# Projections of retention heads one to five as 2x2 blocks from seven products

## Chip, core and metric

One core of one Trainium2 chip. The metric is the device time of one launch in microseconds. Engines are named as in the profile: PE is TensorE (PEld its weight loads), DVE is VectorE, ACT is ScalarE, POOL is GpSimd, SP is SyncE, which here issues the DMAs.

## What is computed

A trunk of two layers over 1024 tokens of width 1024, all in float32. Layer 0 mixes tokens by retention (six heads of width 128), layer 1 by neighbourhood attention; in both, four memory heads of width 64 attend to 256 memory tokens. Each layer ends in a feed-forward part. The change lies in the input projection of layer 0:

```python
proj = a @ w_in                      # a: 1024 x 1024, normed tokens
q, k, v, g, mq = jnp.split(proj, [768, 1536, 2304, 3072], axis=-1)
qh = rotary(to_heads(q, 6), pos)
kh = rotary(to_heads(k, 6), pos) * 128 ** -0.5
vh = to_heads(v, 6)
# forward and backward scans over chunks of 128 tokens, with a decay per head
y = retention(qh, kh, vh, log_gamma[0]) + flipped retention(..., log_gamma[1])
y = group_norm(y) * gn_g + gn_b      # per head and token
y = silu(g) * y
m = memory_attention(mq, mem_k, mem_v)
return jnp.concatenate([y, m], axis=-1) @ w_out
```

## The kernel before

**Matmuls.** A float32 product is made of three fp32r matmuls (`three`, L2321 to L2325): high part by high, high by low, low by high. A high part is a rounded copy, made on ScalarE; the low part is the rest, made on GpSimd or VectorE.

**Units.** The projection goes in units: a unit n is 128 output features, its weight tile `stage[:, n % 3, :]` has 1024 columns (eight k tiles of 128). SyncE loads it (`load_units`, in a ring of three), ScalarE makes `whi` (`split_hi`), GpSimd `wlo` in two halves (`split_lo`, L929). `project(n, k)` multiplies it with k tile k of the tokens `aT` (th: token half 0 or 1, hi or lo), into one PSUM bank per token half. A unit is 8 x 2 x 3 = 48 matmuls of 512 columns. Units `U_RETH + 4h` to `+ 4h + 3` are query, key, value and gate of retention head h.

**Stages.** First the memory keys and values, then the memory queries. Then the memory attention of layer 0, in 19 steps (`mem_step`): sixteen tiles of 128 tokens and head pair go through scores, maxima (DVE, `memory_peaks`), exponentials (ACT), normalising (DVE, L2014), transposes (PE, L2596), copy (ACT) and product with the values. Between them TensorE works off the 32 k tiles of head 0's four units. VectorE also builds the decay tables there (`decays`) and rotates head 0's query and key.

**The head loop.** For h = 1 to 5 TensorE does: unit q of head h; `chunk_scores(h)`, which turns keys and values of head h-1 to token rows and makes its chunk scores; unit k; `chunk_states(h)`; unit v; `chunk_outputs(h)`; unit gate; `turn_outputs(h)`. All work of one head's chunks thus has a unit of the next head beside it. VectorE: `rotate` (query; four instructions per token half, the first three read PSUM), `values` (V and the decayed scores ST), `rotate` (key), `scan` (14 state updates), `take_scaled` (value), `group_norm`, `take_gate`, `gated_values`. ScalarE: the high parts, `Ktok` and `vfb` (keys and decayed values by rows), `Silu` of the gate, gain and offset of the group norm. GpSimd: the low parts, the decayed queries `qfb` (L1104) and the factors of the group norm.

**Order of the work.** It is written out by hand for each engine, in its own instruction queue; semaphores join them. There is no planner. An engine stops at each wait, and whatever is queued behind the waiting instruction stops with it.

**Room.** SBUF is full. `whi` and `wlo` (24 KB of a partition) are free while no unit is in them. After the last head `out_rows` begins the output projection, with the parts of the concatenation split in `cat_split`; heads 0 and 1 of it are split early, into `catE`.

Of the kernel before, what the change touches and what calls it, by code (L numbers as in the profile page):

```python
# [62 lines left out]


# [34 lines left out]
def trunk_program(nc, wpack, w1, w2, x, mem, x_cols, mem_cols, gains, gain_rows, gn, decay, rpb, ropes, decay_consts, na_masks, ident_c, out):  # L99
# [9 lines left out]
    memkv_dram = nc.dram_tensor("memkv_scratch", [P, 1536], F32).ap()  # L109
# [75 lines left out]
    W = X + 64 * KB  # L185
    W += 6 * KB
    bdK = at("bdK", [P, 2, 2 * MEM], F32, W + 53 * KB)
    memV = at("memV", [P, 2, 2 * P], F32, W + 57 * KB)
# [3 lines left out]
    ropeC = at("ropeC", [P, SEQ], F32, W)  # L192
    ropeS = at("ropeS", [P, SEQ], F32, W + 4 * KB)
    QD = at("QD", [P, 2, RH, P], F32, W + 8 * KB)
    DM = at("DM", [P, RH, P], F32, W + 14 * KB)
    qT = at("qT", [P, 2, SEQ], F32, W + 17 * KB)
    kT = at("kT", [P, SEQ], F32, W + 25 * KB)
    Ktok = at("Ktok", [P, 8, P], F32, W + 29 * KB)
    V = at("V", [P, 8, P], F32, W + 33 * KB)
    ST = at("ST", [P, 8, P], F32, W + 37 * KB)  # L200
    vT = at("vT", [P, SEQ], F32, W + 41 * KB)
    states = at("states", [P, 8, 2, P], F32, W + 45 * KB)
    catE = at("catE", [P, 2, 2, HALF], F32R, Z + 24 * KB)
    rawE = at("rawE", [P, 2, HALF], F32, Z + 32 * KB)
    rtmp = at("rtmp", [P, HALF], F32, Z + 36 * KB)
    dconst = at("dconst", [P, 6, P], F32, Z)
    dexp = at("dexp", [P, 2, P], F32, Z + 3 * KB)
    mvT = at("mvT", [P, 2, MEM], F32, W + 49 * KB)
    junk_first = at("junk_first", [P, D], BF16, W + 51 * KB)
    xraw = at("xraw", [P, 2, KD, HALF], F32, W + 17 * KB)  # L210
    memraw = at("memraw", [P, KD, MEM], F32, Z + 16 * KB)
    xrow = at("xrow", [P, SEQ], F32, X + 64 * KB)
    junk_dve = at("junk_dve", [P, D], BF16, Z + 34 * KB)
    memA = at("memA", [P, 2, KD, MEM], F32R, W)
    memrow = at("memrow", [P, MEM], F32, X + 68 * KB)
# [10 lines left out]
    with ExitStack() as ctx:  # L226
# [22 lines left out]
        s_in = [sem(f"s_in{r}") for r in range(6)]  # L249
        b_in = [[sem(f"b_in{b}_{c}") for c in range(3)] for b in range(4)]  # L250
# [5 lines left out]
        cat_ld = [[sem(f"cat_ld{th}_{k}") for k in range(KD)] for th in range(2)]  # L256
        cat_hi, cat_lo = sem("cat_hi"), sem("cat_lo")
# [8 lines left out]
        k_last = sem("k_last")  # L266
        v_mm, v_ea, v_ed = sem("v_mm"), sem("v_ea"), sem("v_ed")
# [18 lines left out]
        for n in range(4 * RH):  # L286
            taken_by(U_RETH + n, "d")
# [53 lines left out]
        def cat_source(l, th, k):  # L341

            if (l, th) == (0, 0) and k < 2:
                return rawE[:, k, :]
            return catf[:, k, HALF * th:HALF * th + HALF]
# [11 lines left out]

        RUN_A0 = (0, 16, 0, 0)
# [13 lines left out]
        def unit_bank(n):  # L372

            return 2 * (n % 2) + (4 if U_RETH + 4 <= n < U_OUT0 else 0)
# [74 lines left out]

        USED, count = {}, 0  # L450
        for n in range(U_END):
            for l in range(2):
# [86 lines left out]
        def s_come(l, q):  # L539
            return 16 * ((13, 13, 13, 13, 13, 12)[s_slot(q)] * l + q // 6 + 1)  # L540
# [9 lines left out]
        def _(sp):  # L550
            issued = [0]

            def load_units(upto):

                for n in range(issued[0], min(upto, U_END)):
                    if n >= RING:
                        sp.wait_ge(w_lo, n - RING + 1)
# [59 lines left out]
            def out_phase(l):  # L617

                U, e = U_OUT[l], 16 * l
                if l == 0:  # L620
                    load_units(U + 9)
                    sp.wait_ge(*USED[U + 4])
                    for i in range(2, TT):
                        load_h(i)
# [16 lines left out]
            def before_out(l):  # L641

                sp.wait_ge(oc_rdy, 16 if l else 2)
                for i in range(TT if l else 2):
                    load_h(16 * l + i)
                if l:
                    load_gain(2 * l)
                    return
                for k in range(2):
                    sp.wait_ge(oc_st[k], stored(k))  # L650
                    sp.dma_start(rawE[:, k, :], cat_dram[0, k, :, 0:HALF]).then_inc(cat_ld[0][k], 16)
# [6 lines left out]
            def cat_back(l, th, tiles, free=None):  # L658

                cols = slice(HALF * th, HALF * th + HALF)  # L660
                sp.wait_ge(*(free or USED[U_OUT[l] - 1]))
# [26 lines left out]
            def load_w1(l, m):  # L688

                if m < RING:  # L690
                    sp.wait_ge(w_lo, U_OUT[l] + 2 * KD - 2 + m)
                else:
                    w1_freed(l, m - RING)
# [109 lines left out]
            sp.dma_start(memkv_dram[:, 0:1024], bdK[:, :, :].rearrange("p a c -> p (a c)")).then_inc(mkv_st, 16)  # L803
            sp.dma_start(memkv_dram[:, 1024:1536], memV[:, :, :].rearrange("p a c -> p (a c)")).then_inc(mkv_st, 16)
# [8 lines left out]
            before_out(0)  # L813
            load_units(U_RETH + 4 + 5)
            for h in range(1, RH):
                load_units(U_RETH + 4 * h + 4 + 5)
                if h == 4:
                    sp.wait_ge(cat_lo, 2)
                    load_gain(0)
                if h == RH - 1:  # L820
                    cat_back(0, 0, range(2, KD - 2))
# [27 lines left out]
            sp.dma_start(bdK[:, :, :].rearrange("p a c -> p (a c)"), memkv_dram[:, 0:1024]).then_inc(mkv_ld, 16)  # L849
            sp.dma_start(memV[:, :, :].rearrange("p a c -> p (a c)"), memkv_dram[:, 1024:1536]).then_inc(mkv_ld, 16)  # L850
# [64 lines left out]
        def _(pool):  # L915
# [8 lines left out]
            def split_lo(n, slot, need):  # L924
                pool.wait_ge(w_hi, need)
                width = w_cols(n).stop // 2
# [6 lines left out]
            def los(upto):  # L933

                for n in range(done[0], min(upto, U_END)):
                    if n in (FIRST_LO, U_NA + 2):
                        pool.wait_ge(w_lo, n)
                    split_lo(n, w_slot(n), n + 1)
# [143 lines left out]
            pool.memset(bdK[:, :, :], 0.0).then_inc(zer, 1)  # L1082
# [10 lines left out]
            for h in range(RH + 1):  # L1093
                n = U_RETH + 4 * h
                los(min(n + 3, U_OUT0 + 2))
                if h == RH:
                    los(U_OUT0 + 3)
                if h:

                    pool.wait_ge(kv_mm, h)  # L1100
                    pool.wait_ge(*EV[n - 4])
                    pool.wait_ge(dec_e, 3)
                    for d in range(2):
                        ins = pool.tensor_tensor(qfb[:, d, :].rearrange("p (a c) -> p a c", a=8),  # L1104
                                                 qT[:, (h - 1) % 2, :].rearrange("p (a c) -> p a c", a=8),
                                                 QD[:, d, h - 1:h, :].to_broadcast([P, 8, P]), ALU.mult)
                    ins.then_inc(qfb_rdy, 1)
                    los(min(n + 5, U_OUT0 + 2) if h < RH else U_OUT0 + 4)

                    for b in range(2):  # L1110
                        four = slice(4 * b, 4 * b + 4)
                        pool.wait_ge(var_rdy, 2 * h - 1 + b)
                        link(pool.tensor_scalar(gvar[:, four], mv[:, four, 1], 1.0, 1e-5, ALU.mult, ALU.add))
                        pool.tensor_tensor(grstd[:, four], gvar[:, four], minus_half[:, four], ALU.pow).then_inc(grs_rdy, 1)
                if h < RH:
                    los(n + 6)
# [44 lines left out]
        def _(act):  # L1161
# [8 lines left out]
            def his(upto):  # L1170

                for n in range(done[0], min(upto, U_END)):
                    if U_NA <= n < U_NA + RING:
                        act.wait_ge(g_used, (71, 72, 73)[w_slot(n)])
                    split_hi(n, w_slot(n), w_come(n), USED[n - RING] if n >= RING else None)
# [206 lines left out]
            def out_hi(l, q):  # L1382
# [11 lines left out]
                if p in "123":  # L1394
                    act.wait_ge(b_in[BLOCK_OF[p]][k // 4], 16 * (l + 1))
# [89 lines left out]
            def cat_split(l, pieces):  # L1485

                for piece in pieces:
# [5 lines left out]
                    else:  # L1493

                        act.wait_ge(cat_ld[th][k], 16 * (l + 1))
# [41 lines left out]
            def take_value_gate(h, i):  # L1537

                n = U_RETH + 4 * h + i
                his(n + 3)  # L1540
                if i == 3:
                    act.wait_ge(*EV[n])
                    act.activation(OC[:, h % 2, :], OC[:, h % 2, :], ACT.Silu).then_inc(ev_act, 1)


            for t in range(steps(RUN_A0)):
                mem_step(RUN_A0, t)
                decays(t)
                for u in units_done(t, 4 * KD, steps(RUN_A0)):
                    take_value_gate(0, u)  # L1550
            for h in range(1, RH + 1):
                n = U_RETH + 4 * h
                g = h - 1
                if h < RH:
                    his(n + 3)
                for b in range(2):
                    act.wait_ge(ktr, 2 * h - 1 + b)
                    act.activation(Ktok[:, 4 * b:4 * b + 4, :].rearrange("p a c -> p (a c)"),
                                   PS[:, (4 if h == RH else 0) + b, :], ACT.Copy).then_inc(ktok_rdy, 1)
                act.wait_ge(vtr, h)  # L1560
                if h == 1:
                    act.wait_ge(dec_rdy, 2 + RH)
# [6 lines left out]
                if h < RH:  # L1569
                    his(n + 4)  # L1570
                    take_value_gate(h, 2)
                    if h == 3:
                        cat_split(0, range(2))
                    take_value_gate(h, 3)
# [1369 lines left out]
```

## Time and profile before

| | us |
|---|---|
| median of 3 runs (2225.1 to 2225.68) | 2225.38 |
| span of the profiled execution | 2224.7 |
| PE busy | 2211.3 |
| DVE busy | 1228.9 |
| POOL busy | 1086.9 |
| ACT busy | 889.0 |

The profiled execution has no time of its own beside its span; the median of the runs lies 0.7 us above that span. PE's busy time counts overlapped matmuls as modelled, so 99% says that it hardly ever waits and not that it can go no faster. The granted clock is full in all slices of the page. The memory attention of layer 0 lies at about 47 to 119 us, head 1 begins at 119 us, and the key transposes of the last head at 399 us.

### The profile page before, as it was taken

How to read it: one execution, taken by the hardware profiler on the slowest of the kernel's cores; microseconds unless marked ns; L12 is line 12 of the kernel's file. 1: busy time of each engine (PE TensorE's matmuls, PEld its weight loads, DVE VectorE, ACT ScalarE, POOL GpSimd, SP SyncE). 2: the span in 40 equal slices, each digit the busy share in tenths (PEclk: the TensorE clock that was granted, in tenths of full speed). 3: DMA queues.
4: the chain of work that ended last, by engine and by line, in shares of the span. 5: the costliest groups of instructions: out<-in, count | busy, mean ns of one | idle time of the engine just before them, and what ended most of it. 6: DMA issues, size and time to landing. Idle time of an engine off the chain costs nothing.

```text
span 2224.7 us, 31738 instructions
## 1 busy us (share of the span) xinstructions
PE 2211.3 (99%) x11662; PEld 1820.2 (82%) x11662; DVE 1228.9 (55%) x2075; ACT 889.0 (40%) x1775; POOL 1086.9 (49%) x881
## 2 busy tenths in 40 slices
PE   9999999999999999999999999999999999999998
PEld 8788888888888888888889877768878888888887
DVE  6744454647644444577763245555575344447767
ACT  6621111455232333344564345565732323324444
POOL 1133333478988888400325243416799888870001
PEclk9999999999999999999999999999999999999999
DMA  8021111443443333663363533234433433238334
GB/s 335 29 86 48 48 48 58 141 162 108 149 147 114 100 110 104 218 218 98 91 203 113 140 83 81 66 131 161 161 114 126 149 100 114 95 124 321 95 97 164
DMA packets 130968, 280.89 MB, mean 126 GB/s; under 512 B 31983, under 2 KB 46590, under 8 KB 128766
## 3 DMA queue, kind: packets, MB, share of 16 engines
q1 hardware_dynamic: 130814, 278.86, 37.6%
q8 instruction: 94, 1.54, 0.3%
q14 instruction: 60, 0.49, 0.1%
HBM read 208.03 MB, written 70.80 MB: 125 GB/s over the span
## 4 chain that ended last, share of the span: by engine, by line
PE 94%; POOL 3%; ACT 1%; DVE 1%; issue 1%; DMA 0%; SPq 0%; POOLq 0%; DVEq 0%; ACTq 0%
PE PS L2323 28%; PE PS L2325 28%; PE PS L2324 28%; PE PS L2596 2%; POOL OPS L993 2%; PE PS L2834 2%; PE PS L2816 1%; PE PS L2733 1%; PE PS L2583 1%; PE PS L2629 1%; POOL TW L1017 1%; PE PS L2720 0%; PE PS L2744 0%; PE PS L2748 0%; PE PS L2746 0%
## 5 line engine op out<-in xcount | busy, mean ns | idle before, releaser
L2323 PE MATMUL PS<-AOP,OPS 128*128 128x512 f32 x1216 | 474.5, 390 | 1.1 <-POOL OPS L993 0.6
L2325 PE MATMUL PS<-AOP,OPS 128*128 128x512 f32 x1216 | 473.4, 389 | 0.0
L2324 PE MATMUL PS<-AOP,OPS 128*128 128x512 f32 x1216 | 473.3, 389 | 0.0
L929 POOL TENSOR_TENSOR wlo<-stage,whi 128x512 fp32r<-128x512 f32 (+1 forms) x160 | 203.1, 1292 | 312.7 <-ACT whi L1168 312.5
L993 POOL TENSOR_TENSOR OPS<-TW,OPS 128x512 fp32r<-128x512 f32 x174 | 263.2, 1527 | 78.9 <-ACT OPS L1266 77.6
L2323 PEld LDWEIGHTS PS<-AOP,OPS 128*128 128x128 f32 x1216 | 228.3, 188 | 51.2 <-POOL OPS L993 2.4
L2325 PEld LDWEIGHTS PS<-AOP,OPS 128*128 128x128 f32 x1216 | 228.3, 188 | 47.5
L2324 PEld LDWEIGHTS PS<-AOP,OPS 128*128 128x128 f32 x1216 | 228.3, 188 | 47.1
L2323 PE MATMUL PS<-aT,whi 128*128 128x512 f32 x640 | 261.7, 409 | 0.0
L2325 PE MATMUL PS<-aT,wlo 128*128 128x512 f32 x640 | 250.6, 391 | 0.0
L2324 PE MATMUL PS<-aT,whi 128*128 128x512 f32 x640 | 249.7, 390 | 0.0
L1266 ACT ACTIVATE OPS<-TW 128x512 fp32r<-128x512 f32 x176 | 106.6, 628 | 343.9 <-POOL TW L1017 321.3
L2323 PE MATMUL PS<-OPS 128*128 128x512 f32 x584 | 227.8, 390 | 0.3
L2325 PE MATMUL PS<-OPS 128*128 128x512 f32 x584 | 227.3, 389 | 0.0
L2324 PE MATMUL PS<-OPS 128*128 128x512 f32 x584 | 227.3, 389 | 0.0
L993 POOL TENSOR_TENSOR OPS<-stage,OPS 128x512 fp32r<-128x512 f32 x128 | 178.3, 1396 | 48.5 <-ACT OPS L1266 40.8
L944 POOL TENSOR_SCALAR msq<-sumsq 128x1 f32<-128x1 f32 x32 | 21.2, 662 | 349.5 <-ACT junk L1188 348.3
L1826 DVE TENSOR_TENSOR up<-PS,u 128x512 f32<-128x512 f32 x88 | 60.8, 691 | 219.3 <-PE PS L2325 218.0
L1393 ACT ACTIVATE OPS<-SRAW 128x512 fp32r<-128x512 f32 x146 | 92.3, 632 | 196.4 <-PE PS L2325 196.4
L1168 ACT ACTIVATE whi<-stage 128x1024 fp32r<-128x1024 f32 (+1 forms) x88 | 90.3, 1029 | 171.3 <-PE PS L2325 164.8
L1858 DVE TENSOR_TENSOR OPS<-SRAW,OPS 128x512 fp32r<-128x512 f32 x146 | 100.7, 690 | 88.3 <-ACT OPS L1393 88.1
L2325 PEld LDWEIGHTS PS<-aT,wlo 128*128 128x128 f32 x640 | 120.1, 188 | 26.3
(259 smaller groups left out, 4139.2 us busy)
## 6 DMA issues: line engine op xcount, KB each, us to landing
stage<-in_w SPq DMA_DIRECT2D x100, 512.0 KB, 4.0
hidden_scratch<-HT SPq DMA_DIRECT2D x154, 256.0 KB, 2.2
SRAW<-hidden_scratch SPq DMA_DIRECT2D x154, 256.0 KB, 2.6
stage<-in_wpack SPq DMA_DIRECT2D x76, 512.0 KB, 3.9
BW<-in_w SPq DMA_DIRECT2D x16, 1024.0 KB, 7.9
h_scratch<-Hb SPq DMA_DIRECT2D x24, 512.0 KB, 3.5
Hb<-h_scratch SPq DMA_DIRECT2D x24, 512.0 KB, 5.8
cat_scratch<-OC SPq DMA_DIRECT2D x14, 512.0 KB, 3.0
```

What stands on the lines that cost most here:

```text
L929: ins = pool.tensor_tensor(wlo[:, slot, cols], stage[:, slot, cols], whi[:, slot, cols].bitcast(F32), ALU.subtract)
L993: pool.tensor_tensor(place[:, 1, :], w1_operand(l, j, p), place[:, 0, :].bitcast(F32), ALU.subtract)\
L1168: act.activation(whi[:, slot, w_cols(n)], stage[:, slot, w_cols(n)], ACT.Copy).then_inc(w_hi, 1)
L1266: act.activation(op_place(q)[:, 0, :], w1_operand(l, j, p), ACT.Copy).then_inc(o_hi, 1)
L1393: act.activation(s_op[:, 0, :], SRAW[:, s_slot(q), :], ACT.Copy).then_inc(g_hi, 1)
L1826: dve.tensor_tensor(dst, PS[:, in_bank(l, j, p), :], with_, ALU.add).then_inc(f_ed, 1)
L1858: dve.tensor_tensor(place[:, 1, :], src, place[:, 0, :].bitcast(F32), ALU.subtract).then_inc(g_lo, 1)
L2323: pe.matmul(dst, stat[0], mov[0], start=start, stop=False, skip_group_check=onto)
L2324: pe.matmul(dst, stat[0], mov[1], start=False, stop=False, skip_group_check=onto)
L2325: return pe.matmul(dst, stat[1], mov[0], start=False, stop=stop, skip_group_check=onto)
L2596: ins = pe.transpose(PS[0:keys, banks(r)[1], c * P:(c + 1) * P], SB[:, r % 3, c * width:c * width + keys], ident[:, :])
L2834: ins = pe.matmul(PS[half, 7, slot:slot + GW], Vc[0:keys, g % 2, place, half], PT[0:keys, r % 3, col:col + GW], start=(c == 0), stop=(c == ...
```

## The change

For each head h = 1 to 5, query and key are one pair of units, value and gate another (r = 0 to 9). A pair is a 2x2 block product: rows are the halves of the contraction, columns the two units, and the tokens are taken as two halves too. Seven block products replace eight. They need sums of weight blocks, sums of token blocks, and sums of the products.

```diff
+RET_ORDER = "1627543"
+RET_PLACE = {"1": 0, "2": 0, "6": 1, "7": 2, "4": 2, "5": 3, "3": 3}
...
+            def block_product(q):
...
+                for k in range(4):
...
+                    ins = three(ret_bank(p), (place[:, 0, c], place[:, 1, c]), (ret_tokens(p, 0, k), ret_tokens(p, 1, k)),
+                                k == 0 and p in "1675", k == 3, p in "243")
```

TensorE's order. `block_product` waits for its low part, and "4" for sum "u3", "3" for sum "22"; a first product of the next pair waits for the bank's last sum.

```diff
             for h in range(1, RH):
-                n = U_RETH + 4 * h
-                if h == 1:
-                    pe.wait_ge(s_exp, 16)
-                unit(n)
+                q = 14 * (h - 1)
                 chunk_scores(h)
-                if h == 1:
-                    pe.wait_ge(pt_ev, 16)
-                    pe.wait_ge(o_ev, o_count(16))
-                unit(n + 1)
+                for i in range(3):
+                    block_product(q + i)
                 chunk_states(h)
-                unit(n + 2)
+                for i in range(3, 7):
+                    block_product(q + i)
                 chunk_outputs(h)
-                unit(n + 3)
+                for i in range(7, 11):
+                    block_product(q + i)
                 turn_outputs(h)
+                for i in range(11, 14):
+                    block_product(q + i)
```

VectorE's order in a head (`product_sum` adds a PSUM bank to a block in SBUF; `turn_pairs` rotates 512 tokens in four instructions, its source is PSUM in `query_first` and SBUF in the three others):

```diff
+                values(h)
...
+                    product_sum(r, "u2")
+                    block_lo(r)
+                    scan(h, lambda c: product_sum(r, "u3") if c == 3 else None)
+                    product_sum(r, "22")
+                    query_first(r)
+                    key_second(r)
+                    product_sum(r, "21")
+                    product_sum(r, "12")
                     group_norm(h)
+                    product_sum(r + 1, "u2")
+                    query_second(r)
+                    block_lo(r + 1)
+                    value_first(r + 1)
+                    product_sum(r + 1, "u3")
+                    key_first(r)
+                    product_sum(r + 1, "22")
+                    gated_values(h)
+                    product_sum(r + 1, "21")
+                    value_second(r + 1)
+                    gate_part(r + 1, "22")
+                    product_sum(r + 1, "12")
+                    gate_part(r + 1, "12").then_inc(c_sum, 1)
```

GpSimd makes the weight sums ("5", "6", "7", "4") and six of seven low parts of a pair; ScalarE all high parts, four products ahead, and copies product "1" out of its bank (`first_product`):

```diff
+            def first_blocks(r):
+                weight_sum(r, "5")
+                weight_sum(r, "6")
+                block_lo(7 * r)
+                block_lo(7 * r + 1)
+                weight_sum(r, "7")
+                block_lo(7 * r + 2)
...
+            for h in range(1, RH):
+                q = 14 * (h - 1)
+                block_lo(q + 3)
+                weight_sum(2 * h - 2, "4")
+                block_lo(q + 5)
+                if h == 1:
+                    for k in range(4):
+                        token_lo_late(k)
+                query_decays(h)
+                block_lo(q + 6)
+                first_blocks(2 * h - 1)
+                group_factors(h)
+                block_lo(q + 10)
+                weight_sum(2 * h - 1, "4")
+                block_lo(q + 12)
+                block_lo(q + 13)
+                if h < RH - 1:
+                    first_blocks(2 * h)
```

The token sums are made once, in steps 1 to 9 of the memory attention, from the raw tokens that stay in SBUF:

```diff
+            def token_sums(t):
...
+                if 1 <= t < 5:
...
+                    link(dve.tensor_scalar(xraw[:, 1, 4 + k, :], xraw[:, 1, 4 + k, :], g2, None, ALU.mult))
+                    dve.scalar_tensor_tensor(out=xraw[:, 1, 4 + k, :], in0=xraw[:, 1, k, :], scalar=g1,
+                                             in1=xraw[:, 1, 4 + k, :], op0=ALU.mult, op1=ALU.add).then_inc(s_one, 1)
+                if 3 <= t < 7:
...
+                if 6 <= t < 10:
```

(two more such instructions for each t of 3 to 6, one for each t of 6 to 9). GpSimd makes a difference and a low part for each of four k tiles there, ScalarE two high parts in each of steps 4 to 7; eight more high parts follow on ScalarE at the stage's end and in head 1, with four low parts on VectorE (`first_sum_lo`) and four on GpSimd (`token_lo_late`).

Moved besides: SBUF places (rotation tables, retention tiles, memory tables); the memory key table loses its zero half; the key transposes use banks 4 and 5 in every head; heads 0 and 1 of the concatenation are loaded and split at the end of head 5 and not in head 3; gain and residual for the first output load after the last `turn_outputs`; the next units' loads wait for the last read of a raw block; some semaphores are shared with the feed-forward stage.

## Rows read from the trace of the kernel before

**Rows 1.** The page: busy us of each engine, share of the span, instructions.
```profile
PE 2211.3 (99%) x11662; PEld 1820.2 (82%) x11662; DVE 1228.9 (55%) x2075; ACT 889.0 (40%) x1775; POOL 1086.9 (49%) x881
```

**Rows 2.** TensorE timeline of one unit: start, us, engine, line, operation.
```profile
219.51 0.39 PE L2325 MATMUL PS<-aT,wlo 128*128 128x512 f32 x1
...
229.72 0.39 PE L2325 MATMUL PS<-aT,wlo 128*128 128x512 f32 x1
```

**Rows 3.** Windows of one head: us, busy of PE, PEld, DVE, ACT, POOL; clock; DMA.
```profile
185.70:241.70 56.00, 56.00 (x293) 48.01 (x292) 27.10 (x64) 9.91 (x13) 17.64 (x14) 1.00 0.14 48
```

**Rows 4.** Windows of the memory attention, steps 2 to 9, two in each; same columns.
```profile
52.90:59.43 6.53, 6.39 (x35) 4.95 (x35) 3.85 (x14) 3.10 (x11) 0.00 (x0) 1.00 0.27 80
59.43:68.32 8.89, 8.89 (x56) 6.92 (x56) 6.77 (x17) 8.40 (x27) 1.50 (x2) 1.00 0.01 2
68.32:75.85 7.53, 7.53 (x51) 5.76 (x50) 7.12 (x18) 4.54 (x14) 1.06 (x1) 1.00 0.22 70
75.85:83.34 7.49, 7.49 (x51) 5.76 (x50) 6.33 (x20) 4.54 (x14) 0.00 (x0) 1.00 0.00 0
```

**Rows 5.** Waits of TensorE up to 430 us: us in total, times, longest.
```profile
PE PS L2645 <- POOL kprod L1083: 1.9, 1, 1.9
```

**Rows 6.** VectorE by line and shape, feed-forward stage: busy us, mean ns, idle before.
```profile
L1838 DVE TENSOR_TENSOR HT<-sg,up 128x512 f32<-128x512 f32 x20 | 34.4, 1721 | 0.0
L1826 DVE TENSOR_TENSOR up<-PS,u 128x512 f32<-128x512 f32 x38 | 26.3, 691 | 98.0 <-PE PS L2325 97.5
```

**Rows 7.** VectorE timeline at the start of the memory attention.
```profile
50.34 0.68 DVE L2117 TENSOR_TENSOR ropeC<-ropeC,xrow 128x512 f32<-128x512 f32 x1
51.06 1.66 DVE L2117 TENSOR_TENSOR ropeS<-ropeS,xrow 128x512 f32<-128x512 f32 x1
```

**Rows 8.** GpSimd timeline of the same time.
```profile
49.11 3.06 POOL L929 TENSOR_TENSOR wlo<-stage,whi 128x512 fp32r<-128x512 f32 x2 [4.39 <-ACT whi L1168]
```

**Rows 9.** One line each: ns min/median/max, first and last start.
```profile
L1688 DVE SCALAR_TENSOR_TENSOR aT<-xraw,gT,aT x16: 742/745/752, 15.4 to 30.9; 128x512 fp32r<-128x512 f32 x16
...
L929 POOL TENSOR_TENSOR wlo<-stage,whi x48: 1277/1288/1719, 116.6 to 425.4; 128x512 fp32r<-128x512 f32 x48
```

**Rows 10.** VectorE timeline of one head.
```profile
185.98 0.69 DVE L2061 TENSOR_TENSOR qT<-PS,ropeC 128x512 f32<-128x512 f32 x1 [7.37 <-PE PS L2325]
...
188.86 0.69 DVE L2061 TENSOR_TENSOR qT<-PS,ropeC 128x512 f32<-128x512 f32 x1
...
206.44 0.35 DVE L2188 SCALAR_TENSOR_TENSOR states<-states,cdec,PS 128x128 f32<-128x128 f32 x1
...
210.55 0.34 DVE L2191 SCALAR_TENSOR_TENSOR states<-states,cdec,PS 128x128 f32<-128x128 f32 x1
...
216.79 0.89 DVE L2205 BATCH_NORM_STATS2 stats<-PS 128x6 f32<-128x128 f32 x4 [1.17 <-PE PS L2748]
...
220.47 1.33 DVE L2213 TENSOR_SCALAR ST<-PS,mv,grstd 128x128 f32<-128x128 f32 x4
```

**Rows 11.** TensorE timeline: chunk states of one head, transposes of another.
```profile
200.17 3.20 PE L2733 MATMUL PS<-vfb,Ktok 128*128 128x128 f32 x16
...
398.86 1.04 PE L2703 MATMUL PS<-ident,kT 128*128 128x128 f32 x8
399.73 1.04 PE L2710 MATMUL PS<-ident,vT 128*128 128x128 f32 x8
```

**Rows 12.** VectorE and TensorE timeline: a normalised row and its transposes.
```profile
71.58 0.62 DVE L2014 TENSOR_SCALAR SB<-SB,rowinv 128x256 f32<-128x256 f32 x2
...
75.33 0.60 PE L2596 MATMUL PS<-ident,SB 128*128 128x128 f32 x4
```

**Rows 13.** DMA issue (page: KB, us to landing), last turn of outputs, first use of gain.
```profile
Hb<-h_scratch SPq DMA_DIRECT2D x24, 512.0 KB, 5.8
...
L2756 PE MATMUL PS<-ident,ST x48: 270/272/273, 173.9 to 427.5; 128*128 128x128 f32 x48
...
440.54 2.47 DVE L1716 TENSOR_TENSOR Yb<-PS,gB 128x512 f32<-128x512 f32 x4
```

More of the change, by code:

```diff
@@ L285, in trunk_program @@
             taken_by(U_RET + n, "a")
-        for n in range(4 * RH):
+        for n in range(4):
             taken_by(U_RETH + n, "d")
@@ new lines, in ret_weight, with ret_lo_done @@
+        def ret_weight(q):
+            r, p = ret_op(q)
+            if p in "123":
+                slot = w_slot(ret_units(r)[1 if p == "3" else 0])
+                return stage[:, slot, 0:HALF] if p == "1" else stage[:, slot, HALF:2 * HALF]
+            return ret_sum(p)
+        def ret_lo_done(q):
+            r, i = q // 7, q % 7
+            if RET_ORDER[i] == "5":
+                return q_lo_dve, r + 1
+            return q_lo, 6 * r + len([p for p in RET_ORDER[:i + 1] if p != "5"])
@@ new lines, in weight_summed, with summed @@
+        def weight_summed(p, r):
+            return q_sum, 4 * r + "5674".index(p) + 1
+        SUMMED = {}
+        for h in range(1, RH):
+            a, b = 2 * h - 2, 2 * h - 1
+            for item in (("u2", a), ("u3", a), ("22", a), ("11", a), ("21", a), ("12", a), ("u2", b), ("query", h), ("11", b),
+                         ("u3", b), ("key", h), ("22", b), ("21", b), ("value", h), ("12", b), ("gate", h)):
+                SUMMED[item] = len(SUMMED) + 1
+        def summed(what, n):
+            return c_sum, SUMMED[what, n]
@@ L620, in out_phase @@
                 if l == 0:
+                    load_units(U + 7)
+                    sp.wait_ge(y_tr, 2 * RH)
+                    load_gain(0)
+                    for i in range(2):
+                        load_h(i)
                     load_units(U + 9)
-                    sp.wait_ge(*USED[U + 4])
                     for i in range(2, TT):
@@ new lines, in group_factors @@
+            def group_factors(h):
+                for b in range(2):
+                    four = slice(4 * b, 4 * b + 4)
+                    pool.wait_ge(var_rdy, 2 * h - 1 + b)
+                    link(pool.tensor_scalar(gvar[:, four], mv[:, four, 1], 1.0, 1e-5, ALU.mult, ALU.add))
+                    pool.tensor_tensor(grstd[:, four], gvar[:, four], minus_half[:, four], ALU.pow).then_inc(grs_rdy, 1)
+            for k in range(4):
+                token_diff(k)
+            los(U_RETH + 3)
@@ L1585, in _ @@
                                    scale=gnT[:, 0, g:g + 1], bias=gnT[:, 1, g:g + 1]).then_inc(aff, 1)
+                if h < RH - 1:
+                    block_hi(q + 15)
+                    block_hi(q + 16)
+                elif h == RH - 1:
+                    act.wait_ge(*summed("query", h))
+                    act.wait_ge(*summed("key", h))
+                    cat_split(0, range(2))
             out_phase(0)
```

525 lines of the change are left out of this document (374 added, 151 removed).

## Prediction

> **What bounds the kernel now.** I read the page first. TensorE is busy 99% of the span and no other engine above 55% [rows 1], so only less TensorE work or a new wait of TensorE can move the time. Next the timeline of its matmuls in one unit, because a matmul's row (0.39 us) is longer than the step from one to the next: 45 steps from 219.51 to 229.72 us, so 0.227 us each [rows 2]. Then the stretch by windows, to see which engine is second. One head takes 56.0 us with TensorE full, VectorE busy 27.1 us of it and GpSimd 17.64 [rows 3]. In the memory attention it is otherwise: VectorE is busy 6.77 of 8.89, 7.12 of 7.53 and 6.33 of 7.49 us [rows 4]. Last, the waits of TensorE up to 430 us: the longest is 1.9 us, at the start, and none lies in the heads [rows 5]. So the heads have much room on paper and the memory stage almost none.
>
> **What TensorE is spared.** A pair of units (q with k, v with gate) is 96 matmuls now; seven products of 12 are 84. Ten pairs save 120 matmuls, 120 x 0.227 = 27.2 us, and a head's full-TensorE period falls from 56.0 to 50.5 us. The chunk work of a head (12.4 us, 56.0 less 192 x 0.227) stays. If nothing waited, the result would be 27 us less.
>
> **A price that decides: VectorE beside GpSimd.** VectorE reading PSUM and one SBUF tile takes 691 ns while GpSimd is at work; the same shape with two SBUF operands takes 1721 ns on average in the worst line [rows 6]. The timelines show the rule exactly. GpSimd makes half of a wlo in 1.28 us undisturbed [rows 9], two would be 2.5. From 49.11 us on they take 3.06. VectorE's first two-operand instruction comes at the end of the first half (50.34, 0.68 long), the second half starts after it, and VectorE's next one, 51.06 + 1.66 = 52.72, ends 0.55 us after the second half (52.17) [rows 7, 8]. So each holds the other off for a whole instruction, and where both have a queue they alternate: up to 1721 - 691 = 1.03 us lost per VectorE instruction with two SBUF operands.
> The Trainium skill (GPSIMD Engine Reference, section Specifications) says the same of the engines: GpSimd's SBUF interfaces are shared with VectorE, in contention with VectorE instructions that have two SBUF inputs or use a two-port mode. The trace agrees (691 against 1721 ns). Without that rule the sum below would end near 2211 us, with it near 2237.
>
> **The new head.** GpSimd gets eight weight sums and twelve low parts, 20 x 1.29 = 26 us [rows 9], besides the decays of the queries; before it had eight halves (10.3 us). VectorE gets ten product sums and two low parts; it loses none of its rotations, and three of the four quarters now read their block from SBUF. I followed the five queues of instructions in program order with these durations (the walk). The longest circle goes: states matmuls end; on VectorE the scan, 4.45 us (206.44 to 210.55 and one more); four half rotations of 2.88 (185.98 to 188.86); statistics 2 x 1.3 (0.89 and the aggregate); normalising 2 x 1.4; nine single instructions (sums, one low part, the first value block) of 0.69; in all 27.6 us [rows 10]. The last of them, sum "22" of the second pair, releases product "3". Then TensorE: that product 2.72, two sets of transposes 2 x 0.87, scores 16 x 0.11 = 1.8, three products 8.17, states 2.95 (3.20 with the tail of the last) [rows 11], two handovers of 0.2 (estimated: 0.39 less the step of 0.227): 17.8 us. Together 45.4, under 50.5: with no contention TensorE stays full.
> But 14 instructions of this circle have two SBUF operands (one of the first query half, four each of the second key, second query and first key halves, one low part). If they lose more than 50.5 - 45.4 = 5.1 us together, TensorE waits. Bounds of the loss: 0 and 14 x 1.03 = 14.4 us. Placing them beside GpSimd's queue: the second key half runs against a low part, sums "5" and "6" of the next pair and its first low parts, 4.1 us; the second query half meets the low parts of "4" and "3" only at its end, 2.3; the first key half meets the next head's sums, 4.1. With 0.2 at the first query half this is 10.7 us, and the circle is 56.1 us: all of the saving is given back. In time, TensorE would stand 1.9 us before the second pair's product "5" (its low part is VectorE's, late behind the query rotation) and 3.6 before its "3". The first heads are still catching up and the last has no next head's weights: 3.0, 4.3, 5.5, 5.5 and 1.9 us, sum 20.2.
>
> **Entering the heads.** Before, the q unit of head one (10.9 us) stood between the memory stage and the key transposes and covered everything. Now the transposes come at once: the value transposes wait for the gate's eviction (0.4), product "1" for the key copies, which stand on ScalarE behind four token high parts and the value transposes (1.7), "6" for its low part behind the sums "5" and "6", which can start only when unit gate leaves its slot (2.1), and "3" for a low part behind four token parts and the query decays on GpSimd (2.3). Sum 6.6 us; between 2 and 10.
>
> **Token sums under the memory attention.** VectorE gets four tensor_scalar and 16 scalar_tensor_tensor of 128x512 in steps 1 to 9. The latter cost 745 ns [rows 9]; the first lie between 0.31 and 0.62 (one and two of the 128x256 kind in rows 12), I take 0.42. That is 13.6 us, and GpSimd's eight new instructions add waits, about 3 us. Idle time of VectorE in steps 2 to 9 is 2.7 + 2.1 + 0.4 + 1.2 = 6.4 us [rows 4], of which links and waits for ScalarE leave some 3.5 usable. TensorE needs VectorE's peaks and normalised rows in the next step: the row made at 71.58 to 72.20 is turned at 75.33, a slack of 3 us [rows 12], though the walk shows the order of ScalarE (its token high parts ahead of the next exponentials) using most of it up. So TensorE stands 16.6 - 3.5 = 13 us, less if the slack helps; I take 12.5, ends 5 and 17. Nothing later hides it: TensorE is full behind.
>
> **The rest.** First output rows wait for the split of heads 0 and 1 of the concatenation, moved behind the last gate: 0.7 us. The weights of a pair are on chip before their sums in the walk. Residual and gain now load only after the last turn at 427.5 us; the gain's first use is at 440.5 and a tile of the residual lands in 5.8 us [rows 13]: covered, and 5 us of play. Semaphores shared and smaller memory tables cost nothing on a path.
>
> **Sum.** -27.2 + 20.2 + 6.6 + 12.5 + 0.7 = +12.8 us. My walk of the old memory stage comes out 2% short, so there TensorE gives more cover than I counted: 1.2 less, +11.6. Profiled span 2224.7 + 11.6 = 2236; the median of the runs lies 0.7 above the span: **2237 us**.
>
> **Rivals.**
> - *Not alternating.* GpSimd's instructions often wait for ScalarE, so VectorE may meet it half as often: 14 x 0.55 = 7.7 us, circle 53.1 against 50.5. The heads then keep some 13 of 27 us, entry and memory stage cost 6 and 9: about +2, 2227 us. Chance 0.15.
> - *The heads run full (the other side).* If the losses of a circle stay under 5.1 us, the 27.2 remain; less 5 for the entry and 8 for the memory stage, whose excess is there without contention: 2211 us. For it: the circle has 5 us of play, and the feed-forward stage has the same scheme with TensorE full. Against it: there VectorE has two to five such instructions per seven products, here 18 per fourteen, four in a row. Chance 0.26, with the case below.
> - *Memory stage also covered*, through slack over several steps: 2200 us, 0.05 of those 0.26.
> - *The granted clock falls* in the new waits of TensorE of 2 to 4 us. All windows read 1.00, but none holds such a wait. Some 10 us of matmuls at half clock would add 10 or more: 2250 us. Chance 0.09.
> - The forecast itself: 0.50, its own range 2229 to 2246.
>
> **Chances.** About 4.5 us (0.2%) is what a measurement can tell from no change. Slower: 0.48 of the forecast, 0.05 of the first rival, 0.09: 0.62. Same: 0.12 (0.10 of the first rival, 0.02 of the forecast). Faster: 0.26, the full heads. Range for 8 in 10: from the full heads to the upper clock case, 2208 to 2250.
>
> **What would show it.** Right: in the profile after, periods from one head's key transposes to the next of 54 to 56 us with TensorE idle 4 to 6 us; "TensorE waited for VectorE" for sum "22" and the low part "5"; rotations of kT from SBUF near 1.7 us each and not 0.7; in the memory stage idle TensorE of about 12 us between steps 5 and 10, released by ScalarE and VectorE. Wrong: periods of 50 to 51 us, rotations near 0.7 us, or memory steps still 7.5 us a pair.

## The result, and the profile after

| | before | after |
|---|---|---|
| median of 4 runs each, same chip (us) | 2225.53 (2225.1 to 2225.75) | 2235.62 (2234.97 to 2237.4) |
| ratio, 95% interval | 1 | 1.0048 (1.0033 to 1.0062) |
| span of the profiled execution (us) | 2224.7 | 2233.2 |

The change makes the kernel 10.1 us slower, 0.45%, though it takes 120 matmuls of 512 columns out of it. The top of the page after:

```profile
span 2233.2 us, 31950 instructions
## 1 busy us (share of the span) xinstructions
PE 2192.5 (98%) x11542; PEld 1799.5 (81%) x11542; DVE 1329.0 (60%) x2159; ACT 923.5 (41%) x1851; POOL 1199.2 (54%) x953
```

Against [rows 1] TensorE has lost busy time, VectorE and GpSimd have gained some 100 us each, and the span is longer. So TensorE must wait now. The waits of TensorE up to 480 us (total, times, longest) say on what:

```profile
PE PS L2692 <- DVE OC L2529: 9.6, 5, 2.1
PE PS L2692 <- DVE wop_b L2536: 6.6, 5, 1.5
PE PS L2954 <- ACT SB L1645: 4.9, 2, 3.1
PE PS L2967 <- ACT PT L1666: 2.8, 2, 2.0
PE PS L2692 <- POOL wop_b L1244: 1.6, 1, 1.6
...
PE PS L2692 <- ACT Ktok L1801: 1.3, 1, 1.3
PE PS L2692 <- POOL wop_a L1244: 1.0, 1, 1.0
```

L2529 is `product_sum`, L2536 VectorE's `block_lo`: each stops TensorE once in each of the five heads. L2954 (scores) and L2967 (transposes) are the memory attention. In [rows 5] none of this is there.

**By stage.** Three marks of TensorE's timeline cut the span: the first memory scores, the first key transposes and those of the last head. The rows of after (start, us; duration), with two more heads between:

```profile
45.97 1.13 PE L2954 MATMUL PS<-bdK_ret,MQ 64*128 64x256 f32 x8
...
129.39 1.09 PE L3100 MATMUL PS<-ident,kT 128*128 128x128 f32 x8
...
188.76 1.03 PE L3100 MATMUL PS<-ident,kT 128*128 128x128 f32 x8
...
243.47 1.03 PE L3100 MATMUL PS<-ident,kT 128*128 128x128 f32 x8
...
406.58 1.03 PE L3100 MATMUL PS<-ident,kT 128*128 128x128 f32 x8
```

| stage (us) | before | after | difference |
|---|---|---|---|
| up to the first scores | 47.33 | 45.97 | -1.4 |
| memory attention, to the end of head 0's last unit | 71.5 | 83.4 | +11.9 |
| heads 1 to 5 (units and chunk work) | 280.1 | 277.2 | -2.9 |
| from the last key transposes to the end | 1825.8 | 1826.6 | +0.8 |
| span | 2224.7 | 2233.2 | +8.5 |

(Before, the q unit of head 1 stood ahead of its key transposes; 48 x 0.227 = 10.9 us are taken off 129.71 for the end of the memory stage, 118.8.) The first line isn't the change's: in the profiled execution of before the clock was down for a while at the start, as the window from 10 to 20 us of before shows (us, busy of PE, PEld, DVE, ACT, POOL, granted clock):

```profile
10.00:20.00 10.00, 9.27 (x65) 9.30 (x66) 8.47 (x14) 7.33 (x14) 0.00 (x0) 0.83 1.03 415
```

After shows 1.00 in the same window, and in all six traces with the new code the first scores come between 45.7 and 46.1 us. So before's own trace held a fall of the clock, which the slices of its page hide: from 12 to 14 us it was 0.50, soon after TensorE had stood 1.80 us (until 10.73 us). The span was 1.8 us under the run's time wherever both are known (2233.2 and 2234.97 in the profiled execution of after), so the profiled execution of before would be about 1 us over its median. Without that line the stages add up to 9.8 us; the medians say 10.1.

**The memory attention.** Windows of after (same columns), two to three steps in each:

```profile
45.97:58.05 12.08, 11.81 (x61) 8.97 (x61) 10.20 (x22) 7.09 (x22) 4.36 (x3) 1.00 0.36 121
58.05:71.13 13.08, 9.12 (x56) 6.88 (x57) 12.65 (x20) 9.79 (x30) 5.87 (x4) 1.00 0.00 1
71.13:84.60 13.47, 9.68 (x50) 6.92 (x51) 12.97 (x24) 6.79 (x19) 5.06 (x5) 0.77 0.12 39
84.60:94.07 9.47, 9.47 (x50) 7.09 (x51) 8.96 (x26) 5.53 (x16) 1.43 (x2) 0.78 0.00 0
```

VectorE is busy 12.65 of 13.08, 12.97 of 13.47 and 8.96 of 9.47 us: it is the bound here (e2 below tests that), where in [rows 4] it still had 0.4 to 2.7 us of play in each window. TensorE stands 3.96 + 3.79 us. And in two windows the granted clock is 0.77 and 0.78. The timeline of TensorE shows the place:

```profile
67.38 0.63 PE L2967 MATMUL PS<-ident,SB 128*128 128x128 f32 x4 [0.84 <-ACT PT L1666]
71.13 1.57 PE L2954 MATMUL PS<-bdK_ret,MQ 64*128 64x256 f32 x8 [3.12 <-ACT SB L1645]
...
73.23 0.63 PE L2693 MATMUL PS<-aT,whi 128*128 128x512 f32 x1
73.65 0.63 PE L2694 MATMUL PS<-aT,wlo 128*128 128x512 f32 x1
74.08 0.63 PE L2692 MATMUL PS<-aT,whi 128*128 128x512 f32 x1
...
81.80 0.99 PE L2967 MATMUL PS<-ident,SB 128*128 128x128 f32 x4 [1.99 <-ACT PT L1666]
84.60 2.08 PE L2954 MATMUL PS<-bdK_ret,MQ 64*128 64x256 f32 x8 [1.80 <-ACT SB L1645]
```

After standing 3.12 us TensorE works at the lower level, 1.2 GHz: a matmul of 512 columns comes every 0.43 us (73.23, 73.65, 74.08) and not every 0.23. At 75 us it is back at 2.4 GHz. It is down once more right behind the next wait, of 1.99 us: the four transposes of 81.80 us take 0.99 us in place of 0.63. It stays down through the wait of 1.80 us that follows, until 88.7 us. Of the 11.9 us of this stage some 7.8 are time stood and the other 4 slower matmuls. The page's row of the clock shows only nines, since its slices are 56 us wide.

**The heads.** The period is 54.7 us (188.76 to 243.47), that of the first head 59.4, that of the last 53.7. VectorE's shapes in heads 2 to 4 of after (busy us, mean ns, idle before):

```profile
L2542 DVE TENSOR_TENSOR kT<-kT,ropeC 128x512 f32<-128x512 f32 x6 | 9.9, 1655 | 0.2
L2541 DVE TENSOR_TENSOR rtmp<-kT,ropeS 64x512 f32<-64x512 f32 x6 | 9.9, 1652 | 0.2
L2543 DVE TENSOR_TENSOR kT<-kT,rtmp 128x512 f32<-128x512 f32 x6 | 9.9, 1644 | 0.2
L2529 DVE TENSOR_TENSOR kT<-PS,kT 128x512 f32<-128x512 f32 x12 | 8.3, 689 | 3.7 <-PE PS L2694 3.7
...
L2542 DVE TENSOR_TENSOR qT<-PS,ropeC 128x512 f32<-128x512 f32 x3 | 2.1, 692 | 0.1
```

The same multiplication takes 692 ns when its block is read from PSUM (the query's first half) and 1655 ns when it is read from SBUF. The two timelines of one stretch show why, VectorE first, then GpSimd:

```profile
213.04 1.60 DVE L2540 TENSOR_TENSOR rtmp<-kT,ropeS 64x512 f32<-64x512 f32 x1
214.67 1.64 DVE L2541 TENSOR_TENSOR rtmp<-kT,ropeS 64x512 f32<-64x512 f32 x1
216.35 1.64 DVE L2542 TENSOR_TENSOR kT<-kT,ropeC 128x512 f32<-128x512 f32 x1
```
```profile
212.34 1.74 POOL L1244 TENSOR_TENSOR wop_b<-stage,wop_b 128x512 fp32r<-128x512 f32 x1
214.05 1.72 POOL L1244 TENSOR_TENSOR wop_a<-wsum_a,wop_a 128x512 fp32r<-128x512 f32 x1
215.73 1.71 POOL L1238 TENSOR_TENSOR wsum_b<-stage 128x512 f32<-128x512 f32 x1
```

Both engines start one instruction about every 1.7 us, in strict turn, and each VectorE instruction ends 0.55 us after a GpSimd instruction has ended (214.67 + 1.64 against 214.05 + 1.72).

### The profile page after: what moved, and what is told of

The parts are those of the page before. It is cut to its first block, busy times and chain, and to the rows that moved or that the text cites. A ratio compares the mean times of both kernels' runs of the same rounds, so it can differ in the third digit from the quotient of the medians.

```text
span 2233.2 us, 31950 instructions
## 1 busy us (share of the span) xinstructions
PE 2192.5 (98%) x11542; PEld 1799.5 (81%) x11542; DVE 1329.0 (60%) x2159; ACT 923.5 (41%) x1851; POOL 1199.2 (54%) x953
## 4 chain that ended last, share of the span: by engine, by line
PE 84%; DVE 6%; POOL 3%; issue 2%; ACT 1%; DMA 0%; DVEq 0%; POOLq 0%; ACTq 0%
PE PS L2692 26%; PE PS L2694 25%; PE PS L2693 25%; PE PS L2967 2%; POOL OPS L1101 2%; PE PS L3233 2%; PE PS L3215 1%; PE PS L3133 1%; DVE rtmp L2540 1%; DVE rtmp L2541 1%; PE PS L3000 1%; PE PS L2954 1%; DVE ST L2471 1%; DVE qT L2542 1%; POOL TW L1125 1%
## 5 line engine op out<-in xcount | busy, mean ns | idle before, releaser
L1035 POOL TENSOR_TENSOR wlo<-stage,whi 128x512 fp32r<-128x512 f32 (+1 forms) x120 | 153.7, 1304 | 218.5 <-ACT whi L1357 218.3
L1125 POOL TENSOR_TENSOR TW<-stage,TW 128x512 f32<-128x512 f32 x88 | 136.5, 1551 | 7.8 <-POOL TW L1125 7.8
L2692 PE MATMUL PS<-aT,whi 128*128 128x512 f32 x320 | 136.2, 426 | 0.2 <-issue 0.2
L2692 PEld LDWEIGHTS PS<-OPS 128*128 128x128 f32 x584 | 109.6, 188 | 23.8 <-DVE OPS L2118 1.1
L2694 PEld LDWEIGHTS PS<-OPS 128*128 128x128 f32 x584 | 109.6, 188 | 22.8
L2693 PEld LDWEIGHTS PS<-OPS 128*128 128x128 f32 x584 | 109.7, 188 | 22.5
```

What stands on the lines that cost most here:

```text
L1035: ins = pool.tensor_tensor(wlo[:, slot, cols], stage[:, slot, cols], whi[:, slot, cols].bitcast(F32), ALU.subtract)
L1125: pool.tensor_tensor(TW[:, TW_OF[p], :], a, b, ALU.subtract).then_inc(t_add[p], 1)
L2692: pe.matmul(dst, stat[0], mov[0], start=start, stop=False, skip_group_check=onto)
L2693: pe.matmul(dst, stat[0], mov[1], start=False, stop=False, skip_group_check=onto)
L2694: return pe.matmul(dst, stat[1], mov[0], start=False, stop=stop, skip_group_check=onto)
```

## The experiments

All have the changed kernel as their base; their times stand beside runs of the kernel before on the same chip, 2225.1 us (e1b and e5: 2225.06). After was timed beside runs of before of 2225.53 us, so a difference to it can be off by about 0.5 us. A stage is read from one profiled execution of each kernel; that of e3 is 2.1 us faster than its median (2223.53 us), those of after, e4 and e5 0.7 us. The stages, cut at the same marks:

| kernel | time | memory attention | heads 1 to 5 | to the end |
|---|---|---|---|---|
| before | 2225.1 | 71.5 | 280.1 | 1825.8 |
| after | 2235.6 | 83.4 | 277.2 | 1826.6 |
| e1b_small_pool | 2217.2 (one run) | 84.1 | 259.3 | 1826.4 |
| e2_no_sums | 2225.5 (one run) | 73.8 | 277.1 | 1826.7 |
| e3_late_sums | 2225.6 | 72.1 | 277.8 | 1825.8 |
| e4_rotate_from_psum | 2222.2 | 83.5 | 264.6 | 1825.9 |
| e5_both | 2211.5 | 72.1 | 265.1 | 1825.8 |

### e1b_small_pool: GpSimd's instructions without their data

```diff
             def block_lo(q):
...
-                pool.tensor_tensor(place[:, 1, :], ret_weight(q), place[:, 0, :].bitcast(F32), ALU.subtract).then_inc(q_lo, 1)
+                if q < 14:
+                    pool.tensor_tensor(place[:, 1, :], ret_weight(q), place[:, 0, :].bitcast(F32), ALU.subtract).then_inc(q_lo, 1)
+                else:
+                    pool.tensor_tensor(place[:, 1, 0:SMALL], rstd[:, 2:2 + SMALL], minus_half[:, 0:SMALL], ALU.pow).then_inc(q_lo, 1)
```

The same for the weight sums; both only from the products of head 2 on (SMALL is 6). A first form, e1_small_pool, with head 1's in it as well, has no result; it expected a period of 50.5 us and 2215 us.

> GpSimd's weight sums and its low parts of the products, from head 2 on (16 to 20 instructions of 128x512 a head), are replaced by as many powers of 128x6 elements in the same places of the queue: these weight sums and low parts are left out of the computation. The matmuls, VectorE's instructions and all waits stay, and so does head 1. Theory (VectorE and GpSimd take turns where both take their inputs from SBUF, and this is what makes VectorE's circle longer than TensorE's): the rotations of VectorE from SBUF, 1.65 us each, fall to about 0.7 us, the period of heads 2 to 4 falls from 54.7 us to 51 to 51.7 us (that of the kernel whose rotations read PSUM was 51.7), and the time by some 13 us to 2222 us. Rival (number and order of VectorE's instructions make the waits, whatever GpSimd does): the period stays at 53.5 us or more and the time at 2230 us or more.

Measured: 2217.21 us, and a period of 50.57 us (the key transposes at 186.75 and 237.32), with no wait of TensorE at all in heads 2 to 4. One head of it, in the window view:

```profile
186.80:237.30 50.50, 50.50 (x269) 43.44 (x268) 34.58 (x76) 15.15 (x25) 34.38 (x27) 1.00 0.17 55
```

GpSimd stays nearly as busy as it was, 34.4 us a head against 37.0: its powers of six elements took 1.32 to 1.43 us on average, about as long as the instructions that they replace when undisturbed, so the same chain of signals runs in about the same time. What is gone is their data: six elements in place of 512 (the operation is another one too). By line, heads 2 to 4, VectorE and then GpSimd:

```profile
L2549 DVE TENSOR_TENSOR kT<-kT,ropeC 128x512 f32<-128x512 f32 x6 | 4.1, 692 | 0.2
L2548 DVE TENSOR_TENSOR rtmp<-kT,ropeS 64x512 f32<-64x512 f32 x6 | 4.1, 686 | 0.2
```
```profile
L1251 POOL TENSOR_TENSOR wop_b<-rstd,minus_half 128x6 fp32r<-128x6 f32 x18 | 25.8, 1431 | 30.3 <-ACT wop_b L1772 30.3
```

The rotation from SBUF falls from 1655 to 692 ns under a GpSimd instruction that is busy just as long. The rival is out: VectorE's number of instructions and their order are the same as in after. The expected period of 51 to 51.7 us and the 2222 us were too careful, the time by 4.8 us: the first head's period fell as well, from 59.4 to 57.0 us, and the last one's to 50.57.

Up to head 1 this kernel is the same as after, but in its profiled execution the clock fell at other moments: 0.50 from 69.5 to 76 us (after: 72 to 75) and from 83.5 to 89.5 us (82 to 88.5). The same waits of TensorE, here:

```profile
70.86 2.08 PE L2961 MATMUL PS<-bdK_ret,MQ 64*128 64x256 f32 x8 [3.12 <-ACT SB L1652]
81.50 0.63 PE L2974 MATMUL PS<-ident,SB 128*128 128x128 f32 x4 [0.99 <-ACT PT L1673]
84.31 2.08 PE L2961 MATMUL PS<-bdK_ret,MQ 64*128 64x256 f32 x8 [2.17 <-ACT SB L1652]
```

With more slow matmuls in front, the wait before the transposes is 0.99 us in place of 1.99, and both scores come as late behind the first scores as in after (25.15 and 38.60 us against 25.16 and 38.63). So up to there slow matmuls took the place of waits. Behind them, where no wait follows, the clock is low for some 5.2 us and not 4.1, and the step is 0.65 us longer (10.12 against 9.47), as is the stage.

### e2_no_sums: the memory attention without VectorE's sums

```diff
             def token_sums(t):
...
-                    link(dve.tensor_scalar(xraw[:, 1, 4 + k, :], xraw[:, 1, 4 + k, :], g2, None, ALU.mult))
-                    dve.scalar_tensor_tensor(out=xraw[:, 1, 4 + k, :], in0=xraw[:, 1, k, :], scalar=g1,
-                                             in1=xraw[:, 1, 4 + k, :], op0=ALU.mult, op1=ALU.add).then_inc(s_one, 1)
+                    dve.engine_nop().then_inc(s_one, 1)
```

The same for the second pair of sums.

> VectorE's sums of token blocks in the memory attention are left out (16 of its 20 instructions are empty, the 4 low parts are copies of one input times zero); GpSimd's differences and low parts, ScalarE's high parts and their waits stay. Part of the computation is left out. Theory (VectorE is the bound of memory steps 1 to 9, and the lost granted clock follows from TensorE's stalls there): the memory stage, from its first scores to the end of head 0's last unit, falls from 83.4 us to 72 to 73 us, the granted clock is full throughout it, and the time falls to about 2225 us. Rival 1 (ScalarE's high parts in its order, or GpSimd's beside VectorE, hold the stage): it stays at 78 us or more, time 2230 or more. Rival 2 (the clock falls for a reason outside VectorE's load): the clock still falls between 68 and 88 us.

Measured: 2225.48 us, the memory stage 73.8 us, clock full. The windows that lie where after lost its time:

```profile
58.05:71.13 13.08, 12.24 (x78) 9.48 (x80) 10.00 (x23) 11.96 (x35) 7.87 (x7) 1.00 0.04 6
71.13:84.60 13.47, 11.92 (x84) 9.25 (x80) 12.89 (x35) 10.38 (x30) 3.61 (x3) 1.00 0.09 34
```

Both rivals are out. About 2.3 us over the stage of before remain with GpSimd's and ScalarE's shares in place (and VectorE's four copies): 9.6 of the 11.9 us are VectorE's own sums and what follows from them. TensorE still stands 0.5 to 1.0 us at a time here, and the clock does not fall.

### e3_late_sums: the same sums, later

```diff
+SUM_A, SUM_B, SUM_HI, SUM_C = [1, 10, 12, 14], [2, 13, 15, 16], [3, 14, 16, 17], [4, 16, 17, 19]
...
-                if 1 <= t < 5:
-                    k = t - 1
+                if t in SUM_A:
+                    k = SUM_A.index(t)
```

The other two groups of sums and ScalarE's high parts (SUM_HI) in the same way; GpSimd's order is moved to match.

> The same token sums, spread over memory steps 1 to 19 in place of steps 1 to 9, most of them behind step 10, where VectorE has slack; GpSimd's first low part moves to fit. Theory (12.5 us of the loss is VectorE's load in steps 1 to 9, and the clock loss hangs on it): the memory stage falls from 83.4 to about 73 us, the granted clock stays full, and the time falls by 10.8 us by a walk through the queues with the measured durations, to about 2225 us, the time before. Rival (the sums cost the same wherever they stand, because the stage as a whole has no slack on VectorE): the time stays at 2233 us or more.

Measured: 2225.61 us, ratio to before 1.000 (0.9991 to 1.001): 10 us better than after, the memory stage 72.1 us; the rival is out. Two windows:

```profile
58.00:71.00 13.00, 12.13 (x76) 9.37 (x78) 11.46 (x24) 10.79 (x32) 3.90 (x3) 1.00 0.07 14
71.00:84.60 13.60, 13.60 (x93) 10.49 (x94) 12.42 (x37) 9.69 (x29) 0.00 (x0) 1.00 0.07 27
```

No sum is left out here; they have only left the steps in which VectorE had no room, and ScalarE's and GpSimd's share has moved with them. The stage is thus 0.6 us longer than before where it was 11.9 longer. Another 0.6 us went into the first head, whose period is 60.0 us against 59.4. That the stage is shorter than e2's, which leaves VectorE's sums out, says that e2's last 2.3 us lay with the place of the other engines' share; which part of it is not shown. With TensorE no longer stopped, its clock is full throughout, so that loss followed from the waits.

### e4_rotate_from_psum: the sums stay in their banks

```diff
-                dve.tensor_tensor(ret_block(r, dst), ret_bank(bank), ret_block(r, with_), ALU.add).then_inc(c_sum, 1)
+                to = ret_bank(bank) if r % 2 == 0 and what in ("21", "12") else ret_block(r, dst)
+                dve.tensor_tensor(to, ret_bank(bank), ret_block(r, with_), ALU.add).then_inc(c_sum, 1)
...
-                turn_pairs(ret_block(r, "21"), ret_block(r, "21"), T1).then_inc(c_sum, 1)
+                turn_pairs(ret_block(r, "21"), ret_bank("4"), T1).then_inc(c_sum, 1)
...
+                elif r % 2 and p in "75":
+                    pe.wait_ge(*summed({"7": "query", "5": "key"}[p], h))
```

The key's first half likewise from bank "3". VectorE's order changes with it: the query's second half is rotated right behind its sum, the key's second half after both, and the second pair's low part of "5" comes later.

> In the query and key pair the last two sums ('21' and '12') are written into their PSUM banks in place of SBUF, and the second half of the query and the first half of the key are rotated from PSUM (0.7 us an instruction in place of up to 1.65 us beside GpSimd); the next pair's products '7' and '5' then wait for the rotations. Theory (VectorE's circle in the heads is the bound, and its three rotations from SBUF are its dearest part): VectorE loses some 8 us a head, the period of heads 2 to 4 falls from 54.7 to about 51.3 us, and the time by about 16 us to 2220 us; the memory stage stays as it is. Rival (the banks held by the rotations stop TensorE's next products): the period stays within 1 us of 54.7 or grows, time 2235 us or more.

Measured: 2222.16 us, ratio to before 0.9986 (0.9977 to 0.9995), 13.5 us better than after; the period is 51.67 us (187.26 to 238.93). Rows by line of heads 2 to 4:

```profile
L2541 DVE TENSOR_TENSOR rtmp<-PS,ropeS 64x512 f32<-64x512 f32 x9 | 6.2, 693 | 0.3
...
L2544 DVE TENSOR_TENSOR qT<-qT,rtmp 128x512 f32<-128x512 f32 x6 | 6.4, 1064 | 0.2
...
L2579 DVE TENSOR_TENSOR vT<-vT,xrow 128x512 f32<-128x512 f32 x4 | 7.3, 1828 | 0.1
```

and the only wait of TensorE in them:

```profile
PE PS L2693 <- DVE wop_b L2537: 1.6, 3, 0.6
```

The wait for sum "22" is gone, the one for the low part "5" down to 0.6 us. The saving is 2.5 us less than the 16 expected. Part of the lost turns only moved: the multiplication of the value by `xrow` took 693 ns in after and takes 1828 ns here: it starts at 237.20 us, right behind a GpSimd instruction of 237.18 to 238.47, and ends 0.55 us after it. The new waits for banks show nowhere. The rival is out.

### e5_both: e3 and e4 together

> The late token sums and the rotations from PSUM together, nothing left out. Theory (the two causes are independent: VectorE in the memory stage with the clock loss, VectorE's circle in the heads): the savings add up, 11.5 us of span by the one and 13.5 us by the other, so the time is 2235.6 - 25 = 2210.6 us, 14.5 us under the kernel before, ratio 0.9935. Rival (the same slack was used twice: with a shorter memory stage the entry into head 1 waits for the last token low parts): the time is 2216 us or more.

Measured: 2211.53 us (2210.79 to 2212.11), ratio to before 0.9939 (0.9926 to 0.9953). The stages are those of e3 and of e4 (72.1 and 265.1 us), so the two causes are independent (the rival's 2216 us is not reached), and this version beats both kernels: 13.5 us under before, 24 under after. Its waits of TensorE up to 480 us, the large ones:

```profile
PE PS L2696 <- DVE wop_b L2540: 3.9, 5, 1.7
PE PS L2696 <- POOL wop_b L1245: 1.6, 1, 1.6
...
PE PS L2696 <- ACT Ktok L1804: 1.3, 1, 1.3
PE PS L3116 <- DVE OC L2394: 1.1, 1, 1.1
...
PE PS L2696 <- POOL wop_a L1245: 1.0, 1, 1.0
```

Most of what is left is the entry into head 1, whose period is still 58.6 us, 8 over the full one.

## Why the prediction was right, step by step

- **What TensorE is spared, 27.2 us: right.** e1b's heads without a wait have the period 50.57 us, where 56.0 less 24 x 0.227 is 50.55.
- **The price that decides, alternation: right, and shown.** In after the two engines take turns one for one. e1b takes away GpSimd's traffic and leaves its time, and 1655 ns fall to 692.
- **The circle in the heads: right in kind, a little high.** The period was to be 54 to 56 us and is 54.7. Over 50.57 the heads 2 to 5 lose 4.1, 4.1, 4.1 and 3.1 us, in sum 15.5; forecast were 17.2. The two waits came where they were named, the low part "5" (forecast 1.9 us, measured 1.5 at most) and the sum "22" (3.6 against 2.1). Together these are 3.6 us of a head's 4.1: a wait's row counts from the end of the matmul's 0.39 us record and not from its step of 0.227 (0.16 us), and the first matmul behind it takes a longer step (185.92 to 186.22, 240.62 to 240.93 and 396.87 to 397.21: 0.07 to 0.11 us more), so each wait costs some 0.25 us more than its row says. The sign "TensorE idle 4 to 6 us" a head was missed by this: the rows say 3.6. Head 5 was mis-sized the other way: it was to lose 1.9 us.
- **Head 1 and the entry: right.** Forecast 6.6 us for the entry and 3.0 for the head, 9.6 together; measured 59.4 - 50.6 = 8.8. (The four terms of the entry add up to 6.5 and not 6.6.) All four waits named are there, one a little larger and three smaller: 0.5 for the gate's eviction (forecast 0.4), 1.3 for the key copies (1.7), 1.6 for the low part of "6" (2.1), 1.0 for that of "3" (2.3). The head's own two add 0.7 and 2.1; with 0.25 for each of the six this makes 8.7.
- **Token sums under the memory attention, 12.5 us: right in size, one part of it unforeseen.** 11.9 measured. The sum counted time stood alone, and its sign was 12 us of idle TensorE; 7.8 us were that and some 4 were matmuls at 1.2 GHz. Of these, the slow matmuls ahead of the second pair of waits took the place of waits: e1b shows it, with more of them and as much less waiting. Those behind the last wait (84.60 to 88.7 us, about 2 us lost) have no wait after them. VectorE is busy 8.96 of that window's 9.47 us, so by an estimate at most 0.5 us of them came on top; no kernel here has the waits without the clock, and this part stays open. VectorE's 20 instructions took 15.7 us and not 13.6, mostly because four of them (L2503) took 1.20 us each and not 0.745.
- **The rest, 0.7 us: near.** The wait for the split of heads 0 and 1 is 0.48 us, at 408.97 us. The stage's 0.8 is not its measure: with the same move e3, e4 and e5 have 1825.8 or 1825.9 us, as before has.
- **The 1.2 us taken off** for the walk's shortness in the memory stage fits it (12.5 less 1.2 is 11.3), but the larger part of what the sum had too much lay in the heads: 26.8 us of waits forecast, 27.2 - 2.9 = 24.3 measured.
- **The total.** The sum was +11.6 us; the stages that the change touches say +9.8, the medians +10.1. The forecast's base, 2224.7 + 0.7 = 2225.4 us, was right because two things outside the change offset each other: the profiled execution of before had lost time at its start, about 1 us by its span, and a run's time stands 1.8 us over the span of such an execution, not 0.7.

Of the rivals, *the heads run full* is what e1b shows, and what e5 comes near to, with heads of 51.6 us. That e5's 2211.5 us meets the rival's 2211 is chance: its first head loses 8.1 us and the other four 4.2 together, where that sum had 5 us in all, and its memory stage 0.6 and not 8. As the change stands, VectorE's losses in a circle are past the 5.1 us at which it decides. *Not alternating* was wrong. *The granted clock falls* did happen, in the memory attention and not in the heads, and with 4 us in place of 10: in the heads TensorE stood 2.1 us at most at a time, and the clock read 1.00 there. The rival named waits of 2 to 4 us as a danger that no row held; before's wait of 1.80 us at its start, with the clock at 0.50 behind it, was such a case and was not among the rows.

## What to carry to other kernels

A sum of busy time doesn't say whether two engines fit side by side: ask of each VectorE instruction whether it has two SBUF operands while GpSimd has a queue, and if so count GpSimd's instruction with it. In e4 such an instruction got its speed back (0.69 us for 1.65) by leaving one operand in PSUM, though the bank is then held longer. Work that is put under a stage costs nothing only in those of its steps in which the engine that does it has room: the same 20 instructions of VectorE (some 15 us) made the memory attention 11.9 us longer in steps 1 to 9, and 0.6 us when most of them stood in steps 10 to 19.

## What the runs showed of the hardware

- That GpSimd is busy by the profile is not enough to make VectorE take turns. Powers of 128x6 elements occupied GpSimd for 1.32 to 1.43 us on average, as long as an addition of 128x512, and VectorE's instructions with two SBUF operands kept their 0.69 us under them. That the small traffic is the reason is likely and not isolated, since the powers are also another operation. The Trainium skill (SBUF — State Buffer, section "SBUF: two separate sides") says that the pair of ports is held "for the whole instruction"; for GpSimd's small powers, which read SBUF too, this case does not show that; its strict turns with 128x512 additions and subtractions fit it.
- VectorE's instructions with one operand in PSUM and one in SBUF took 674 to 694 ns on average in heads 2 to 4 of after and of e4, also where they stood beside a full GpSimd queue (e4, 212.37 to 214.50 us: 0.68 and 0.69 us each, GpSimd's instruction of 212.84 us beside them 1.27).
- In after the granted clock was at the 1.2 GHz level behind a wait of 3.12 us and again right behind one of 1.99 us; in before it fell about 1 us after the end of one of 1.80 us. It stayed at 2.4 GHz through waits of 2.11 to 2.15 us in the heads. So the length of the last wait alone does not tell; and the same instructions lost the level from 69.5 us in one execution (e1b) and from 71.5 us in another (after). At the lower level a matmul of 512 columns came every 0.43 us.
